# Centred output weights, k's lengths from a diagonal, and narrow projections side by side, in a four-layer block on one core

## The reference

```python
def second_block(x, ...):
    for i in range(2):
        if i == 0: y = gdn_mixer(x, ...)     # gated delta rule, 8 heads
        else:      y = gla_mixer(x, ...)     # gated linear attention, 4 heads
        x = layer_norm(DEEP_ALPHA * x + y, ln_g[i], ln_b[i])

def gdn_mixer(x, w_in, conv_w, a_log, dt_bias, norm_w, w_out):
    p = x @ w_in                                      # q, k, v, gate and 16 columns beta, alpha
    qkv = causal_conv_silu(p[..., :GDN_QKV], conv_w)
    q, k = l2norm(q), l2norm(k)                       # t * rsqrt(sum(t*t) + 1e-6)
    beta = sigmoid(b_logit); g = -exp(a_log) * softplus(a_logit + dt_bias)
    o = gated_delta_rule(q, k, v, g, beta)
    return gated_rmsnorm(o, norm_w, gate).reshape(...) @ w_out
```

## Time and profile before

| | us |
|---|---|
| median of 3 runs (2176.34 to 2178.92) | 2177.89 |
| the profiled execution | 2176.11 |
| its span, first to last instruction | 2174.3 |
| TensorE busy | 2106.0 |
| VectorE busy | 1466.0 |
| ScalarE busy | 938.3 |
| GpSimd busy | 53.5 |
| start of the second half (GDN) | 1279 |
| last GDN head | 1832 to 1894 |
| GLA's chains | 1940 to 2142 |

### The profile page before, as it was taken

How to read it: one execution, slowest core, us unless ns; L and a number is a source line. 1 busy time by engine, 2 the same in 40 slices (tenths; PEclk the granted TensorE clock), 3 DMA queues, 4 the chain that set the end, 5 groups by cost and what they waited for, 6 DMA issues and landing times. The chain is left out here.

```text
span 2174.3 us, 37825 instructions
## 1 busy us (share of the span) xinstructions
PE 2106.0 (97%) x15297; PEld 1817.6 (84%) x15297; DVE 1466.0 (67%) x2880; ACT 938.3 (43%) x1808; POOL 53.5 (2%) x33
## 2 busy tenths in 40 slices
PE   8998999999999999999999999999999999899996
PEld 8996667899988977889998888887888788688885
DVE  5258875988755777498886455666665666675567
ACT  5236872555400467355550024433443343355443
POOL 1110000000000300000000000000000000000000
PEclk9999999999999999999999999999999999899998
DMA  5230001233232210122323212111111210212211
GB/s 183 95 115 21 2 2 59 99 106 106 100 117 85 107 73 21 58 88 98 114 91 118 95 68 78 59 56 61 58 42 55 77 39 0 95 42 95 78 40 39
DMA packets 30666, 159.37 MB, mean 73 GB/s; under 512 B 3392, under 2 KB 3904, under 8 KB 17856
## 3 DMA queue, kind: packets, MB, share of 16 engines
q1 hardware_dynamic: 30240, 157.24, 20.4%
q10 hardware_dynamic: 288, 0.20, 0.0%
HBM read 155.33 MB, written 2.10 MB: 72 GB/s over the span
## 5 line engine op out<-in xcount | busy, mean ns | idle before, releaser
L224 PE MATMUL ps<-late_parts,panel_upper 128*128 128x256 f32 (+1 forms) x1392 | 467.0, 335 | 0.0
L223 PE MATMUL ps<-late_parts,panel_upper 128*128 128x512 f32 (+1 forms) x1276 | 441.0, 346 | 4.6 <-DVE xT_sb L3794 2.2
L225 PE MATMUL ps<-late_parts,panel_parts 128*128 128x512 f32 (+1 forms) x1276 | 432.2, 339 | 0.0
L219 DVE TENSOR_TENSOR panel_parts<-panel_sb,panel_upper 128x512 fp32r<-128x512 f32 (+1 forms) x344 | 349.2, 1041 | 14.9 <-ACT panel_upper L723 8.3
L223 PE MATMUL ps<-panel_upper,hT_parts 128*128 128x256 f32 (+2 forms) x964 | 298.7, 310 | 7.3 <-DVE h_lower L911 7.3
L225 PE MATMUL ps<-panel_upper,h_lower 128*128 128x256 f32 (+2 forms) x964 | 285.7, 296 | 0.0
L224 PEld LDWEIGHTS ps<-late_parts,panel_upper 128*128 128x128 f32 x1392 | 263.2, 189 | 26.2 <-issue 0.2
L224 PE MATMUL ps<-panel_parts,hT_parts 128*128 128x256 f32 (+2 forms) x964 | 284.5, 295 | 0.0
L223 PEld LDWEIGHTS ps<-late_parts,panel_upper 128*128 128x128 f32 x1276 | 241.2, 189 | 35.9 <-issue 2.6
L225 PEld LDWEIGHTS ps<-late_parts,panel_parts 128*128 128x128 f32 x1276 | 242.4, 190 | 29.7
L223 PE MATMUL ps<-hT_parts,panel_upper 128*128 128x512 f32 (+1 forms) x508 | 203.4, 400 | 4.1 <-DVE h_lower L3301 2.5
(11 more groups left out here) (513 smaller groups left out, 3706.8 us busy)
## 6 DMA issues: line engine op xcount, KB each, us to landing
panel_sb<-ffn_gate_up_w SPq DMA_DIRECT2D x76, 512.0 KB, 4.5
panel_sb<-gdn_w SPq DMA_DIRECT2D x24, 1024.0 KB, 4.8
panel_sb<-ffn_down_w SPq DMA_DIRECT2D x22, 1024.0 KB, 4.8
panel_sb<-nsa_w SPq DMA_DIRECT2D x13, 1024.0 KB, 6.3
panel_sb<-gla_w SPq DMA_DIRECT2D x12, 1024.0 KB, 4.9
panel_sb<-gdn_out_w SPq DMA_DIRECT2D x8, 1024.0 KB, 4.8
panel_sb<-ffn_gate_up_w SPq DMA_DIRECT2D x6, 1024.0 KB, 4.8
panel_sb<-nsa_out_w SPq DMA_DIRECT2D x4, 1024.0 KB, 4.8
```

Of the source, the lines that this page charges most:

```text
L219: return engine.tensor_tensor(out, src, hi.bitcast(F32), ALU.subtract)
L223: mm(out, w_hi, x_hi, start=start, stop=False, skip_group_check=skip_group_check)
L224: mm(out, w_hi, x_lo, start=False, stop=False, skip_group_check=skip_group_check)
L225: return mm(out, w_lo, x_hi, start=False, stop=stop, skip_group_check=skip_group_check)
```

## The change

Three things. (1) The mean of x is taken out at the start of each mixer instead of near its end: GpSimd sums x (`pool_total`), TensorE spreads the mean in the first stage, ScalarE copies it to SBUF (`act_mean`), and VectorE subtracts it among the first head's steps. For that the output weights of all heads are centred, not only those of the last. The last GDN head's output panel goes to slot 3, and the outputs of head 6 are made in 48 single products, 8 in the first fillings, then 4 and later 3 per place. (2) The lengths of k come from the diagonal of k k^T, which VectorE masks and reduces; these products move into the step section of the head before, into bank 2, and half of the gate moves to bank 3. (3) The upper and lower parts of the 16 columns for beta and alpha stand side by side as 32 columns of weights, with x moving; the result is copied, and turned and added by four small products. The low-rank projection of GLA is done in the same way, with its two parts summed by a doubled second factor.

```diff
 def pe_gdn(pe):
     def beta_alpha():
+        pe.wait_ge(S("g_ba_split"), 1)
+        for k in range(DC):
+            mm(ps[0:BA_ROWS, 0, :], ba_parts[:, k, :], h_hi[:, k, :], start=k == 0, stop=False)
+            last = mm(ps[0:BA_ROWS, 0, :], ba_parts[:, k, :], h_lo[:, k, :], start=False, stop=k == DC - 1)
+        last.then_inc(S("g_ba_rows"), 1)
+    def turn_beta_alpha():
+        pe.wait_ge(S("g_ba_saved"), 1)
         for t in range(TT):
-            for k in range(DC):
-                last = mm(ps[:, 0, t * 16:t * 16 + 16], xT[:, k, t * P:(t + 1) * P], ba_w[:, k, :], start=k == 0, stop=k == DC - 1)
+            last = mm(ps[:, 0, t * 16:t * 16 + 16], ba_rows[:, t * P:(t + 1) * P], ba_pairs, start=True, stop=True)
...
-    def qk_sums(h):
-        pe.wait_ge(S("g_sq"), h * 2 + 2)
-        token_sums(ps[:, 4, 0:TT], [g_sq[:, 0, :]])
-        token_sums(ps[:, 4, TT:2 * TT], [g_sq[:, 1, :]]).then_inc(S("g_ss"), 1)
+    def q_sums(h):
+        pe.wait_ge(S("g_sq"), h + 1)
+        token_sums(ps[:, 4, 0:TT], [q_sq]).then_inc(S("g_ss"), 1)
+    def key_products(h, bank):
+        pe.wait_ge(S("g_silu"), h * 4 + 2)
+        if bank == KK_BANK:
+            pe.wait_ge(S("g_conv"), h * 4 + 4)
+        for t in range(TT):
+            tok = slice(t * P, (t + 1) * P)
+            last = mm(ps[:, bank, tok], conv[1][:, tok], conv[1][:, tok], start=True, stop=True)
+        last.then_inc(S("g_kk"), 1)
...
     def chain(i, p, h):
         def fill(place):
             if h is None:
-                if place < DC:
-                    output(p, place, place + 1)
-                if place == DC + 1:
-                    pe_ln_mean(pe, 0, GDN_MEAN_BANK)
+                start = 8 + 4 * (place - 1) - max(0, place - 8)
+                output_part(p, start, start + (4 if place < 8 else 3))
...
-        pe.wait_ge(S("g_silu"), i * 4 + 2)
-        for t in range(TT):
-            tok = slice(t * P, (t + 1) * P)
-            last = mm(ps[:, 3, tok], conv[1][:, tok], conv[1][:, tok], start=True, stop=True)
-        last.then_inc(S("g_kk"), 1)
...
                 project_gate(h, 0, t and 2 + t, 3 + t)
+                if t == 0:
+                    key_products(h, KK_BANK)
...
     turn_beta_alpha()
-    qk_sums(0)
+    q_sums(0)
+    key_products(0, 3)
     cumulate()
+    pe_ln_mean(pe, 0, GDN_MEAN_BANK)
...
 def act_gdn(act):
                 if l == 4:
-                    upper(GOUT, i)
+                    act.wait_ge(landed[GOUT], (i + act_panels.done[GOUT] + 1) * 16)
+                    act_out_means(act, GOUT)
+                if l == 5:
+                    act_out_upper(act, i, GOUT, "g_out_upper")
+            elif l == 3:
+                act.wait_ge(landed[LAST_OUT], (GH + act_panels.done[LAST_OUT] + 1) * 16)
+                act_out_means(act, LAST_OUT)
+            elif l == 4:
+                act_out_upper(act, i, LAST_OUT, "g_out_upper")
...
 def dve_gdn(dve, link):
-    def variances(h):
-        dve.wait_ge(S("g_ss"), h + 1)
-        nc.vector.tensor_scalar(g_rs, ps[:, 4, 0:2 * TT], L2_EPS, None, ALU.add).then_inc(S("g_var"), 1)
+    def q_variances(h):
+        dve.wait_ge(S("g_ss"), h + 1)
+        nc.vector.tensor_scalar(g_rs[:, 0:TT], ps[:, 4, 0:TT], L2_EPS, None, ALU.add).then_inc(S("g_var"), 1)
+    def key_diagonal(h, bank):
+        dve.wait_ge(S("g_kk"), h + 1)
+        link(nc.vector.tensor_tensor(k_diag, by_tile(bank), spread4(ident[:, :]), ALU.mult))
+    def k_variances(h):
+        link(nc.vector.tensor_reduce(g_rs[:, TT:2 * TT], k_diag, AX_X, ALU.add))
+        nc.vector.tensor_scalar(g_rs[:, TT:2 * TT], g_rs[:, TT:2 * TT], L2_EPS, None, ALU.add).then_inc(S("g_var"), 1)
...
+            elif p is None and place < 4:
+                centre(2 * place)
+                centre(2 * place + 1)
...
+    w, hi, lo = ba_w[:, :, :], ba_parts[:, :, 0:2 * GH], ba_parts[:, :, 2 * GH:BA_ROWS]
+    link(high(hi, w))
+    low(lo, w, hi)
+    nc.vector.tensor_tensor(ba_pairs, ident[0:BA_ROWS, 0:2 * GH], ident[0:BA_ROWS, 2 * GH:BA_ROWS], ALU.add).then_inc(S("g_ba_split"), 1)
     split_panel(dve, link, 2, 0)
...
+def act_mean(act, j, bank):
+    act.wait_ge(S("ln_mean"), j + 1)
+    nc.scalar.copy(ln_total, ps[:, bank, :]).then_inc(S("ln_mean_saved"), 1)
+def pool_total(pool, j):
+    for n in range(1, DC):
+        if n == 1:
+            nc.gpsimd.tensor_tensor(ln_total, xT[:, 0, :], xT[:, 1, :], ALU.add).then_inc(S("ln_total"), 1)
+        else:
+            pool.wait_ge(S("ln_total"), j * (DC - 1) + n - 1)
+            nc.gpsimd.tensor_tensor(ln_total, ln_total, xT[:, n, :], ALU.add).then_inc(S("ln_total"), 1)
...
 def sp_gla(sp):
-    projections(0)
+    for s in range(2):
+        first_projection(s)
     sp.wait_ge(S("g_added"), (GH + 1) * DC)
     sp.dma_start(...)   # the two constant loads
+    first_projection(2)
...
 def act_gla(act):
+        if h is not None:
+            act.wait_ge(landed[OUT], (i + act_panels.done[OUT] + 1) * 16)
+            act_out_means(act, OUT)
         act.wait_ge(S("l_zz"), i * LEVELS + LEVELS - 1)
...
         if h is not None:
-            upper(*out_panel(i))
+            act_out_upper(act, GH + i, OUT, "l_out_upper")
...
 def dve_gla(dve, link):
             out_split(1)
-            for c in range(5):
-                centre(c)
             return
...
     def pool_gla(pool):
+    pool_total(pool, 0)
+    pool.wait_ge(S("l_xscaled"), DC)
+    pool_total(pool, 1)
     for h in range(LH):
         move(h)
```

More of the change, by code:

```diff
@@ L2497, in build_in @@
     nwT = take(TT, P)
-    vnew = [take(GDN_DV) for _ in range(2)]
+    vnew_rows = take(2 * GDN_DV)
+    vnew = [vnew_rows[:, n * GDN_DV:(n + 1) * GDN_DV] for n in range(2)]
     state = take(GDN_DV)
@@ L2634, in output_side, with output_part, output @@
                 last.then_inc(S("g_out"), 1)
-        def output(p, n0, n1):
-            w_hi, w_lo = split_ready(pe, GOUT, p) if n0 == 0 else (hi_ring[GOUT], lo_ring[GOUT])
+        def output_part(p, m0, m1):
+            if m0 == 0:
+                split_ready(pe, GOUT, p)
+            for m in range(m0, m1):
+                n, e, product = m // (3 * VC), m // 3 % VC, m % 3
+                first, final = m % (3 * VC) == 0, (m + 1) % (3 * VC) == 0
+                if first and n >= 2:
+                    pe.wait_ge(S("g_added"), DC + p * DC + n - 1)
+                elif first:
+                    pe.wait_ge(S("g_gate"), (p + 1) * VC + n + 1)
+                if product == 0:
+                    pe.wait_ge(S("g_ysplit"), p * VC + e + 1)
+                w, out = (hi_ring, hi_ring, lo_ring)[product][GOUT], (y_hi, y_lo, y_hi)[product]
+                last = mm(ps[:, PROJ_BANK + n % 2, :], w[:, e * DC + n, :], out[:, e, :], start=first, stop=final)
+                if final:
+                    last.then_inc(used[GOUT] if n == DC - 1 else S("g_out"), 1)
+        def output(p, n0, n1, slot=GOUT):
+            w_hi, w_lo = split_ready(pe, GOUT, p) if n0 == 0 else (hi_ring[slot], lo_ring[slot])
             for n in range(n0, n1):
@@ L2917, in chain @@
                     root(0)
+                if h is not None and t == 1:
+                    norms(h)
             if h is None:
```

195 lines of the change are left out of this document (98 added, 97 removed).

## The result

The changed kernel took 2163.98 us (median of 4 runs, 2161.38 to 2164.80) against 2178.11 us for the kernel before beside it (4 runs, 2176.34 to 2178.92): ratio 0.9935, 95% interval 0.9922 to 0.9947, so 14.1 us faster. The profiled execution took 2164.55 us with a span of 2162.8; beside the 2176.11 us of the profiled execution of before that is 11.6 us less, since that one was at the low edge of its runs and this one near the upper edge of its own.

A forecast was written before the change was run, and what follows sets the result against it. TensorE, busy 2106.0 of 2174.3 us, was taken as the bound: time falls if it does less, idles less or clocks higher. Terms 4.0 + 0.6 - 3.1 - 4.6 - 8.5 - 2.6 = -14.2 us gave 2163.7, called 2163.5; range 2152 to 2173.

The forecast's parts named there:

- GpSimd's company: First GDN stage: GpSimd's additions delay seven VectorE instructions by 0.5 us each, 3.5 us.
- the small instructions: First GDN stage: splitting the new weights puts three small instructions ahead of everything on VectorE, 0.7 us.
- Its bound of 7 x 1.535: First GDN stage: upper bound if each VectorE instruction waits for a whole GpSimd addition, 10.7 us.
- Of the 3.8 us at most 1.2 can be had: First GDN stage: TensorE does 3.8 us less, but the following VectorE and ScalarE chain had only 1.2 us of slack.
- the centrings cost their 0.6 us: First head's steps: the first pair of centrings, 2 x 0.69 us against 0.8 us of slack, costs +0.6 us.
- the rival that ends slower: Step sections: waiting for the fourth convolution starves TensorE and holds the lower clock longer; +20, 2183.6 us; chance 0.04.
- its lower bound: Last GDN head's state steps: 3 us shorter forecast, but only 0.5 if the lower clock comes again.
- the very wait that was forecast: GLA's first chain: ScalarE's new passes delay its copy of the transposed keys, +1.8 us, bounds 0.5 and 3.
- GpSimd blocking one by one: First stage: GpSimd's additions block VectorE individually, costing 10.7 instead of 3.5 us; time 2170.7; chance 0.15.
- Clock falls that stay: Step sections: the clock still falls in four to all seven; time 2168 to 2173; chance 0.17.
- Latency-bound last head: Last GDN head: its level-to-level chain is the bound, gain 2 instead of 8.5 us; time 2170; chance 0.08.
- Better (2155): No collision at the start, no clock fall in any head's steps or at either end; time 2155; chance 0.16.

The follow-up runs named there:

- the run with the plain one: Changed kernel with the 32 plain beta and alpha products back in place of the side-by-side projection: 2156.69 us, ratio 0.9904.
- the late total: Changed kernel, but GpSimd begins its total of x only after VectorE finishes head 0's first convolution: 2160.35 us, ratio 0.9926.
- The run with the late total and the free bank: Changed kernel with GpSimd's total begun late, head 0's third projection in free bank 6, half the fourth projection and mean's product reordered: 2151.23 us.
- the two runs that put eight back and took eight away: Changed kernel with 16 one-column records again: 2172.32 us; kernel before with eight one-column records replaced by one four-column product: 2166.95 us.
- the run with whole outputs: Changed kernel, but the last GDN head does the previous output product in whole outputs at the first eight places: 2167.90 us, ratio 0.9953.
- the additions put back: Changed kernel with additional unused 128x512 VectorE additions in the last GDN head: 2163.45 us, ratio 0.9932.

## Why the prediction was right, step by step

The forecast was 2163.5 us with a range of 2152 to 2173; 2163.98 came. The medians moved by -14.1 us against a sum of -14.2. The pair of traces gives -11.6, of which +1.65 lies ahead of the changed code, so part of the agreement is luck, and the terms show where.

**First stage: +6.6, not +4.** The direction was right, and so were two terms by VectorE's queue: GpSimd's company was put at 3.5 us and cost 3.9, and the small instructions at 0.7 us took that without the company. Its bound of 7 x 1.535 was counted on the wrong engine: what can be delayed is VectorE's exposed instructions, of which there were five, not GpSimd's seven additions. The step that failed is "Of the 3.8 us at most 1.2 can be had": the side-by-side projection stands in the sum with -1.2 us, and the run with the plain one shows that it cost 6.1. The chain from the convolutions to `cumulate` did not keep that slack of 1.2 us, since it runs through the new turned products, and these stand behind `project(0, 2)`, whose bank the first convolution held. `cumulate` began 25.8 us into the stage, not 21.2: +4.6 against the +3.0 that the terms gave. The prediction looked for waits before the q sums and before `cumulate`; the large one, 5.81 us, was ahead of both, at the projection. The mean's product then took 2.1 us, not 1.1, at the lower clock. And the terms don't add, as the prediction had them do: the late total takes off 5.1 us and the plain projection 6.1, each nearly all of the 6.6, so neither is the price of one part beside the other. That a sum of such terms came within 2.6 us is in part luck. The run with the late total and the free bank shows that 11 us of this stage could be had.

**Head 0: +0.9, not 0.** The clock fell once in it (1329.4, 3.4 us), behind the wait of 2.37 us. Where it didn't fall (late total), the same stretch took 76.07 us, 0.1 less than before; so the terms were right in sum but for the clock, and no wait there shows that the centrings cost their 0.6 us.

**Looped heads: -9.9, not -8.2.** Per head without a fall -0.59 against -0.6. All four falls went (6.4 us), not three (4.6). The prediction named the records as what stood before the falls and left open whether fewer of them would do; the two runs that put eight back and took eight away show that fewer of them do. Over the eleven profiled executions with ten or fewer records none of 66 looped heads had a fall; of the twelve with 16, eight had. That the new wait for the fourth convolution would starve TensorE (the rival that ends slower) is refuted: 72.10 busy of 72.14.

**Last GDN head: -7.2, not -7.6.** Levels -3.66 against -3.6: right, and by the pieces, as the run with whole outputs shows. State steps -3.05 against -3, but more by the clock than the prediction says. The prediction names VectorE's splits and centrings first, and the clock only in its lower bound (0.5 us, "if the lower clock comes again"); the additions put back cost 0.7 us there, and the same 36 instructions are busy for 8.58 us at 1.00 instead of 11.36 at 0.73. Some 2.3 to 2.8 us of the 3 are the clock, which is what that bound implies. That it would stay up was luck in part, as the run with the free bank shows, where it fell. The splits themselves were not put back, so their part isn't measured by itself. The end gave 0.5, not 1.

**GLA.** To the first chain -1.4 against -0.9. Chain 0 +1.17 against +1.8, with the very wait that was forecast, on ScalarE's copy; moving two passes takes all of it back. Chains 1 and 2: 0, as said. At the end the 2.20 us wait of the earlier trace rows is gone, -3.9 in the last chain, but the lower clock, of which half was forecast to go, stayed: +0.6.

**The rivals.** GpSimd blocking one by one: that is how it works (each delay under one addition), but over five instructions, so not 10.7 us. Clock falls that stay: no. Latency-bound last head: no, pieces give 3 us. Better (2155): the looped heads and the steps of the last one were without falls as it says, but the collision at the start came, and so did the lower clock at both ends; the version with the free bank goes below its time by another way.

## What to carry to other kernels

TensorE time that is saved ahead of a wait is not saved: find out what the next instruction in its queue waits for, and whether that is data or only a bank that is still being read; here a free bank, with an order that it allows, was worth 6 us with the late total in place. An idle TensorE can be paid twice, when the lower clock follows: of the 11.4 us that the free bank, the new order and the late total gave, 5.4 were busy time. Two costs of one stage don't add where one hides behind the other; take one out at a time before you believe either price. Work put on GpSimd was free only where VectorE wasn't on the path; count VectorE's exposed instructions, at up to one GpSimd instruction each, and look at what the work meets where you move it: the late total met three small instructions again.

## What the runs showed of the hardware that I had not expected

The clock falls without any idle TensorE time: in a looped head that was busy for 74.32 of 74.32 us, and in the looped heads 2.1 to 3.1 us behind the start of 16 one-column records (1.95 us of busy time), in 8 of 12 such heads, and in none of 66 where eight or ten stood there. A fall costs 1.6 us. The same instructions at the same places can fall or not from one execution to the next: the four runs of the free-bank kernel span 7.7 us, with a mean granted clock of 0.987 or 0.991.

GpSimd and VectorE delay each other in both directions: six additions went from 1.34 to 2.36 us each beside VectorE's splits, and a 128-wide two-input instruction of VectorE from 0.29 to 1.41 us, nearly five times. A 2048-wide cast with one input took 1.21 to 1.23 us beside GpSimd in after, as alone, but 1.62 in the run with the plain projection, where it began in the middle of an addition. Measured by their length, small instructions suffer most: 128x32 ones went up from 0.19 to 1.14 us beside the late total.
